# Four gated networks on one NeuronCore: one 512-column product for the high weights, and halves added by VectorE

## The reference

```
ff1, ff2   (d_ff 2816, 22 tiles of 128):  h = (silu(u @ w_gate) * (u @ w_up)) @ w_down
glu1, glu2 (24 tiles of 128):  g = u @ w_gate ;  g' = bias + tap0*g[t-2] + tap1*g[t-1] + tap2*g[t]
                               h = (silu(g') * (u @ w_up)) @ w_down
```

## Time and profile before

| | |
|---|---|
| median of the runs shown | 1355.77 us |
| the profiled execution's own time | 1357.81 us |
| its span in the trace | 1356.0 us |
| TensorE busy | 1320.3 us, 97% |
| VectorE busy | 927.8 us, 68% |
| ScalarE busy | 683.7 us, 50% |
| matmuls | 9752 |
| DMA | 158 GB/s over the span |

### The profile page before, as it was taken

One profiled execution on the slowest core, in us unless ns is written; L12 is line 12 of the kernel. 1 busy time (PEld: TensorE's weight loads), 2 busy tenths in 40 slices (PEclk: granted clock), 3 DMA queues, 4 the chain that ended last, 5 costly groups with the idle time before them and its releaser, 6 DMA issues.

```text
span 1356.0 us, 24418 instructions
## 1 busy us (share of the span) xinstructions
PE 1320.3 (97%) x9752; PEld 1227.8 (91%) x9752; DVE 927.8 (68%) x1458; ACT 683.7 (50%) x1072; POOL 97.2 (7%) x93
## 2 busy tenths in 40 slices
PE   8999999999999999999999999899999999999998
PEld 7999989998799999887999999799998888999997
DVE  5655556768665555687676666699896975766665
ACT  5444446646554444575544444577642544544443
POOL 1000000000000000030000000013201630000000
PEclk9999999999999999999999999999997999999999
DMA  8555544630265555422465555254431114555551
GB/s 317 204 186 183 186 160 146 243 125 1 94 207 186 186 184 186 152 94 96 153 216 186 185 185 185 97 188 159 167 112 63 64 66 152 195 209 186 186 186 63
DMA packets 30603, 214.87 MB, mean 158 GB/s; under 512 B 3648, under 2 KB 3776, under 8 KB 5184
## 3 DMA queue, kind: packets, MB, share of 16 engines
q1 hardware_dynamic: 30096, 212.23, 45.0%
q0 software_dynamic: 432, 1.57, 0.3%
HBM read 212.74 MB, written 1.05 MB: 158 GB/s over the span
## 4 chain that ended last, share of the span: by engine, by line
PE 81%; DVE 13%; ACT 3%; issue 2%; DMA 1%; POOL 0%; SPq 0%; POOLq 0%; ACTq 0%; DVEq 0%
PE bank L497 72%; DVE w_lo L2094 4%; DVE arena L2640 2%; PE bank L806 1%; ACT w_hi L1388 1%; PE bank L854 1%; PE bank L823 1%; DVE arena L2687 1%; DVE par L2685 1%; DMA raw<-weights 1%; PE bank L543 0%; PE bank L1269 0%; DVE xn L2774 0%; DVE stat L2506 0%; PE bank L803 0%
## 5 line engine op out<-in xcount | busy, mean ns | idle before, releaser
L2094 DVE TENSOR_TENSOR w_lo<-raw,w_hi 128x2048 fp32r<-128x2048 f32 x194 | 447.2, 2307 | 186.2 <-ACT w_hi L1388 185.8
L497 PE MATMUL bank<-aT_hi,w_hi 128*128 128x256 f32 x1664 | 472.5, 284 | 2.6 <-DVE w_lo L2094 2.3
L497 PE MATMUL bank<-aT_hi,w_lo 128*128 128x256 f32 x1664 | 470.8, 283 | 0.0
L497 PE MATMUL bank<-aT_lo,w_hi 128*128 128x256 f32 x1664 | 470.8, 283 | 0.0
L1388 ACT ACTIVATE w_hi<-raw 128x2048 fp32r<-128x2048 f32 x198 | 378.0, 1910 | 103.1 <-PE bank L497 99.2
L497 PEld LDWEIGHTS bank<-aT_hi,w_hi 128*128 128x128 f32 x1664 | 319.1, 192 | 4.8 <-DVE w_lo L2094 2.5
L497 PEld LDWEIGHTS bank<-aT_lo,w_hi 128*128 128x128 f32 x1664 | 319.2, 192 | 1.5
L497 PEld LDWEIGHTS bank<-aT_hi,w_lo 128*128 128x128 f32 x1664 | 319.1, 192 | 0.0
L497 PE MATMUL bank<-w_hi,aT_hi 128*128 128x256 f32 (+1 forms) x560 | 172.4, 308 | 5.0 <-DVE aT_lo L2329 4.4
L497 PE MATMUL bank<-w_hi,hT_hi 128*128 128x512 f32 (+1 forms) x432 | 166.2, 385 | 2.9 <-DVE hT_lo L2382 2.9
L497 PE MATMUL bank<-w_lo,aT_hi 128*128 128x256 f32 (+1 forms) x560 | 168.5, 301 | 0.0
(11 more groups left out here) (365 smaller groups left out, 1345.2 us busy)
## 6 DMA issues: line engine op xcount, KB each, us to landing
raw<-weights SPq DMA_DIRECT2D x198, 1024.0 KB, 4.9
post_gain<-post_gains POOLq DMA_DIRECT2D x3, 512.0 KB, 4.1
residual<-x SPq DMA_DIRECT2D x2, 512.0 KB, 4.2
raw<-weights SPq DMA_DIRECT2D x2, 512.0 KB, 7.7
out<-residual SPq DMA_DIRECT2D x2, 512.0 KB, 2.6
par<-params SPq DMA_DIRECT2D x1, 809.0 KB, 10.9
con<-consts SPq DMA_DIRECT2D x1, 520.0 KB, 11.4
con<-consts SPq DMA_DIRECT2D x1, 64.0 KB, 4.4
```

Source lines behind the costliest of these rows:

```text
L497: last = nc.tensor.matmul(to, lhsT, rhs, start=start and n == 0, stop=stop and n == 2)
L2094: nc.vector.tensor_tensor(w_lo[:, i % 3, :], raw[:, i % 3, :], w_hi[:, i % 3, :].bitcast(f32), ALU.subtract).then_inc(w_lo_done, 1)
```

## The change

The high and low activations of a k tile now lie side by side in one buffer, so that 512 adjacent columns hold both. In the tiles of all four networks, a k-step is two products instead of three: the high weights meet all 512 columns, and the low weights meet the 256 high columns. The bank's first half then holds hi*hi + lo*hi, and its second half hi*lo. Gate and up each fill a bank, and two tiles (four banks) are in flight instead of four. VectorE adds the halves of gate and up with a reduction over pairs of numbers that lie 256 apart, and writes gate into `f_tanh` (in glu1 and glu2) or `f_gate` (in ff1 and ff2), and up into `f_hid`. ScalarE and VectorE read them there. Tile 0 of ff2, glu1 and glu2 keeps its form and is copied. Other uses of `aT_hi` and `aT_lo` are unchanged apart from the step between tiles.

```diff
-        aT_hi = sb("aT_hi", [128, 8, SEQ], f32r)
-        aT_lo = sb("aT_lo", [128, 8, SEQ], f32r)
+        aT = sb("aT", [128, 8, 2, SEQ], f32r)
+        aT_hi, aT_lo = aT[:, :, 0, :], aT[:, :, 1, :]
...
+            def both_parts(to, w, k):
+
+                nc.tensor.matmul(to[:, :], w[0], aT[:, k, :, :].rearrange("p a c -> p (a c)"),
+                                 start=k == 0, stop=False)
+                return nc.tensor.matmul(to[:, 0:256], w[1], aT_hi[:, k, :], start=False, stop=k == 7)
...
-                    if f0 + f >= 4:
-                        pe.wait_ge(hid_ready, f0 + f - 3 + 4 * q)
-                    to = bank[4 + f % 4]
+                    if f >= 2:
+
+                        pe.wait_ge(up_sum, f0 + f - 1 + 4 * q)
...
-                            last = exact(to[:, 256 * part:256 * part + 256], weights(i, at, at + 128), left(k),
-                                         k == 0, k == 7)
+                            last = both_parts(bank[4 + 2 * (f % 2) + part], weights(i, at, at + 128), k)
...
-                    gate = bank[4 + f % 4][:, 0:256]
-                    act.wait_ge(item_done, i + 1 + 6 * q)
-                    tanh_of = gate
+                    act.wait_ge(gate_sum, f0 + f + 1 + 4 * q)
                     if conv:
...
-                        nc.scalar.activation(f_gate[:, f % 2, :], gate, ACT.Identity,
+                        nc.scalar.activation(f_gate[:, f % 2, :], f_tanh[:, f % 2, :], ACT.Identity,
...
-                    nc.scalar.activation(f_tanh[:, f % 2, :], tanh_of, ACT.Tanh, scale=0.5).then_inc(gate_tanh, 1)
+                    nc.scalar.activation(f_tanh[:, f % 2, :], f_gate[:, f % 2, :], ACT.Tanh, scale=0.5)\
+                        .then_inc(gate_tanh, 1)
...
-                    gate, up = bank[4 + f % 4][:, 0:256], bank[4 + f % 4][:, 256:512]
-                    g = f_gate[:, f % 2, :]
+                    g, up = f_gate[:, f % 2, :], f_hid[:, f % 2, :]
+                    gate = f_tanh[:, f % 2, :] if conv else g
+                    dve.wait_ge(item_done, i + 1 + 6 * q)
+                    if f == 0 and name in HALVED:
+                        nc.vector.tensor_copy(gate, bank[4][:, 0:256]).then_inc(gate_sum, 1)
+                        nc.vector.tensor_copy(up, bank[4][:, 256:512]).then_inc(up_sum, 1)
+                    else:
+                        sums = [bank[4 + 2 * (f % 2) + part] for part in range(2)]
+                        halves_of = [b[:, :].rearrange("p (a c) -> p c a", a=2) for b in sums]
+                        nc.vector.tensor_reduce(gate, halves_of[0], AX.X, ALU.add).then_inc(gate_sum, 1)
+                        nc.vector.tensor_reduce(up, halves_of[1], AX.X, ALU.add).then_inc(up_sum, 1)
                     if conv:

+                        dve.wait_ge(gate_sum, f0 + f + 1 + 4 * q)
                         dve.wait_ge(gate_scaled, f0 - 44 + f + 1 + 4 * q)
...
+                    dve.wait_ge(up_sum, f0 + f + 1 + 4 * q)
                     nc.vector.scalar_tensor_tensor(f_hid[:, f % 2, :], f_tanh[:, f % 2, :], 0.5, up,
                                                    ALU.mult, ALU.mult).then_inc(hid_ready, 1)
```

More of the change, by code:

```diff
@@ L284, in two_blocks @@
         rows_ready, turned, turned_hi, turned_lo = sem("rows_ready"), sem("turned"), sem("turned_hi"), sem("turned_lo")
+        gate_sum, up_sum = sem("gate_sum"), sem("up_sum")
         gate_scaled, gate_conv, gate_tanh = sem("gate_scaled"), sem("gate_conv"), sem("gate_tanh")
@@ L1406, in turn_out @@
                         last = nc.scalar.activation(
-                            hi[:, 2 * j + k:2 * j + k + step, :].rearrange("p a c -> p (a c)"),
-                            source[:, 256 * k:256 * (k + step)], ACT.Copy, scale=scale(2 * j + k))
+                            hi[:, 2 * j + k:2 * j + k + step, :],
+                            source[:, 256 * k:256 * (k + step)].rearrange("p (a c) -> p a c", c=SEQ),
+                            ACT.Copy, scale=scale(2 * j + k))
                     last.then_inc(turned_hi, 1)
@@ L1452, in tile @@
                         act.wait_ge(gate_conv, f0 - 44 + f + 1 + 4 * q)
-                        tanh_of = f_gate[:, f % 2, :]
-                    nc.scalar.activation(f_tanh[:, f % 2, :], tanh_of, ACT.Tanh, scale=0.5).then_inc(gate_tanh, 1)
+                    nc.scalar.activation(f_tanh[:, f % 2, :], f_gate[:, f % 2, :], ACT.Tanh, scale=0.5)\
+                        .then_inc(gate_tanh, 1)
                     late_split = f == n_tiles - 1
@@ L2121, in turn_out @@
                         last = nc.vector.scalar_tensor_tensor(
-                            lo[:, tiles, :].rearrange("p a c -> p (a c)"), source[:, 256 * k:256 * (k + step)],
-                            scale(2 * j + k), hi[:, tiles, :].rearrange("p a c -> p (a c)").bitcast(f32),
-                            ALU.mult, ALU.subtract)
+                            lo[:, tiles, :], source[:, 256 * k:256 * (k + step)].rearrange("p (a c) -> p a c", c=SEQ),
+                            scale(2 * j + k), hi[:, tiles, :].bitcast(f32), ALU.mult, ALU.subtract)
                     last.then_inc(turned_lo, 1)
@@ L2369, in tile @@
                                                        g[:, 2:256], ALU.mult, ALU.add).then_inc(gate_conv, 1)
-                        gate = g
                     dve.wait_ge(gate_tanh, f0 + f + 1 + 4 * q)
-                    nc.vector.scalar_tensor_tensor(f_tanh[:, f % 2, :], f_tanh[:, f % 2, :], 1.0, gate,
+                    nc.vector.scalar_tensor_tensor(f_tanh[:, f % 2, :], f_tanh[:, f % 2, :], 1.0, g,
                                                    ALU.add, ALU.mult).then_inc(silu_step, 1)
                     dve.wait_ge(silu_step, f0 + f + 1 + 4 * q)
+                    dve.wait_ge(up_sum, f0 + f + 1 + 4 * q)
                     nc.vector.scalar_tensor_tensor(f_hid[:, f % 2, :], f_tanh[:, f % 2, :], 0.5, up,
```

## The result

The changed kernel takes 1379.66 us (median of 4 runs, 1378.58 to 1379.80). The kernel before takes 1355.69 us in the runs beside it (1355.01 to 1356.03). The ratio is 1.0178, 95% interval 1.0165 to 1.0190. So the change makes the kernel slower by 24.0 us; the forecast of 1367.6 us had the sign, and half the size. The time lies above the forecast's own range (1359 to 1374). The whole range (1353 to 1387) holds it only by the end that was drawn for the stepped read, and the stepped read cost nothing.

What follows compares the result with a forecast made beforehand. TensorE bounds the kernel before; after, the VectorE-ScalarE chain bounds glu1 and glu2. Terms glu2 +8.6, glu1 +10.1, ff2 -3.6, ff1 -3.3 sum to +11.8, giving 1367.6 us; own range 1359 to 1374, whole range 1353 to 1387.

Steps and rivals of the forecast that it cites:

- the stepped read: Rival: reductions reading PSUM 256 numbers apart take 1.01 us each; +28 us, 1384 us; chance 0.18.
- The matmul count: Whole kernel: 9752 matmuls fall to 8328, 16 fewer in each of 89 tiles.
- The chain: glu1 and glu2: VectorE and ScalarE's dependent steps become the bound, a pair taking 17.23 us where TensorE needs 16.57.
- The wait for the up sum: glu1 and glu2: tile f waits for tile f-2's up sum, once in each, about 1.2 us at the start.
- 1.57 in the loop and 1.37 outside: glu1 and glu2: us added to each VectorE round by gate sum, hand-overs and L1449, giving 7.51 and 7.19.
- 0.05 for the address it reads from a register in the loop: glu1 and glu2 loops: us added to ScalarE's start after the gate sum, part of the 1.57 a round.
- a tile takes 0.20 us less: TensorE, 89 changed tiles: 5.56 us a tile for 5.75, 17.8 us in all if nothing else got late.
- The 0.77 that I charged to the chain at ff1's end: End of ff1: tile 20's chain to h_lo gets 0.77 us longer, leaving ff1 a gain of 3.3 us.
- The line through two widths: TensorE products: 0.42 ns a column plus 12.5 ns for each product, from 256- and 512-column rows.
- TensorE as the bound: Rival in the glu1 and glu2 loops: at most 1.24 us added a round; -15.9 us, 1339.9 us; chance 0.12.
- The two that cancel: Rival: sums of 0.65 us without register delays, glu1 and glu2 losing 4.5 and 6; +3.6 us or no change; chance 0.08.
- the sum of glu2 along VectorE: glu2: VectorE's rounds and splits added from 1158.50 give 196.9 us, last h_lo at 1355.4, network +8.6 us.

Runs made afterwards that it cites:

- the copy of up: The changed kernel with a 256-wide copy of up's first half in place of up's reduction, leaving out its hi*lo part; 1378.77 us, ratio 1.0160.
- the written-out kernel: The changed kernel with the hardware loops of the four networks written out, so waits and table columns are constants; 1365.16 us, ratio 1.0064.
- the grouped kernel: ff1 and ff2 alone changed, with eight 512-column products before eight 256-column ones in each half tile, where they alternated; 1350.63 us, ratio 0.9960 to the kernel before.

## Why the forecast was wrong, by its steps

**Right.** The matmul count; VectorE busy 1037.8 us (I had 1053, too much by the overlap of back-to-back sums); the reduction at 0.69 (0.686), so the rival of the stepped read is out, which needed 1.01. The chain is the bound of glu1 and glu2, and w_lo and h_lo are what TensorE waits for. L1454 takes 0.60 us from SBUF. The up sum costs nothing (shown by the copy of up). ff1 and ff2 gain (shown by the kernel with them alone). The wait for the up sum bites once in each glu network. In ff1 the table is still loaded beside the last gate sum.

**The step that failed** is "1.57 in the loop and 1.37 outside". Measured: 7.66 - 5.94 = 1.72 and 7.28 - 5.82 = 1.46. Its wrong term is "0.05 for the address it reads from a register in the loop (between 0 and 0.1; no row shows it alone)". ScalarE starts 0.24 us after the sum's end where I had 0.04 + 0.05; 0.24 in the loop and 0.04 in the written-out kernel make the register's share 0.20, outside the bounds I gave. There was a row that should have set the upper bound: I took 0.19 for VectorE's start behind ScalarE in the loop against 0.04 outside, a register's share of 0.15, and gave ScalarE a third of it. The forecast of the mechanism was right; this is a term of its sum that was too small. Outside the loop VectorE starts 0.12 to 0.13 after ScalarE's end (1341.04), where I had 0.04.

In glu2 the miss of 4.0 us is 16 x 0.15 = 2.4 in the loop, 6 x 0.09 = 0.5 outside it, and the first tile at 7.35 for 6.9 = 0.45 (the copies feed ScalarE, and the convolution waits for it once more):

```profile
1167.90 0.42 DVE L2368 COPY arena<-bank 128x256 f32<-128x256 f32 x1
...
1169.41 0.49 DVE L2379 SCALAR_TENSOR_TENSOR arena<-arena,par 128x255 f32<-128x255 f32 x1 [0.76 <-ACT arena L1454]
...
1175.25 0.68 DVE L2373 TENSOR_REDUCE arena<-bank 128x256 f32<-128x512 f32 x1
```

The last down step adds 0.28: TensorE had waited 3.11 us ahead of it, and its 24 products take 5.74 us in place of the 5.46 of the earlier trace rows.

```profile
1368.48 0.47 PE L498 MATMUL bank<-w_hi,hT_hi 128*128 128x512 f32 x1 [3.11 <-DVE hT_lo L2396]
```

Some 0.4 us of glu2 has no row. In glu1 the first three terms are the same and make its 3.4.

**A second step** was mis-sized: "a tile takes 0.20 us less". It is 5.75 - 5.64 = 0.11 in the order as written. In ff2 this makes 20.5 x 0.09 = 1.8 of the miss of 2.3. In ff1 it makes as much, and only 1.0 was missed, because the network's first product stood 0.73 us earlier, which is luck. The 0.77 that I charged to the chain at ff1's end did come: TensorE waits 3.78 us for the last h_lo, where it waited 2.93.

```profile
193.40 0.77 PE L498 MATMUL bank<-w_hi,hT_hi 128*128 128x512 f32 x1 [3.78 <-DVE hT_lo L2396]
```

The same wait is 2.93 us in both other kernels in which ff1 is the old one and 3.78 to 3.79 in every other kernel that makes both sums there in the alternating order. So ff1's own part is -2.25 by the tiles (20.5 x 0.11) and +0.85 by this wait, -1.4 us for the -3.3 of the forecast. The rest of the -2.3 is the earlier start and 0.2 in the last down step.

The line through two widths gave 5.56 us for a tile; grouped by width a tile is 5.59, and the faster alternating tiles (16 x 346.7 ns = 5.55) meet it. It was drawn through rows in each of which one width stands alone, and most tiles with two widths in turn are slower than it. The Trainium skill ("TensorE: Matmul & The Clock Gate", "Wait — 56ns, not 53.3ns?") gives about 2.5 ns a matmul beside its columns, by which a tile would save 0.04 us; the grouped kernel shows 0.16, and the alternating one 0.11.

**The rivals.** TensorE as the bound needed a round of 7.18 at most; measured 7.66. The two that cancel needed 1.33 a round, without register delays; the written-out kernel has 1.45 there and still loses 9.5 us. The reason is in the sum of glu2 along VectorE: with rounds of 7.27 it ends 5.8 us later than before, and so it does in that kernel's trace, even though the pair (2 x 7.27 + 2.21 = 16.75) is no longer than TensorE's 16.79. VectorE comes late into the network, and with a chain as long as TensorE's pace it never gets ahead again.

## What to carry to other kernels

When work is given from the bound engine to one that seems half idle, ask where in its order the work will stand. Ahead of a step that another engine waits for, 0.27 us a tile cost 10.6 us in all, beside that step about nothing, and moving the same sums to a gap took back 21 of 24 us. Count each hand-over between engines in a hardware loop with its addresses from registers, at the size of the largest one that the trace shows. Change the parts of a kernel apart: here two of four networks gained and two lost.

## What the runs showed that I had not expected

- A dependent step that takes a table column at an address from a hardware loop's register starts about 0.20 us later on ScalarE (0.24 against 0.04 after the releaser's shown end), and 0.06 and 0.12 us later on VectorE. A step whose wait alone takes a register (L1458) starts no later. A round loses 0.38 us, where the chain is the bound.
- Products of 512 and 256 columns in turn, each with its own weights, have two paces in one kernel, 353 and 347 ns a couple, each kept through a tile; eight and eight grouped take 349.4 (5.59 us a tile / 16).
- A reduction over pairs of numbers that lie 256 apart in a bank takes 0.686 us for 512 inputs, the same as one over contiguous numbers (688 ns), although it has 256 outputs and that one 4.
